# Five layer norms kept in PSUM with the modulation products spread around them, and the differential layer's copies and squares moved to ScalarE

## The reference

```python
def layer_norm(x, g, b):
    mu = jnp.mean(xf, axis=-1, keepdims=True)
    var = jnp.mean(jnp.square(xf - mu), axis=-1, keepdims=True)
    y = (xf - mu) * lax.rsqrt(var + LN_EPS) * g + b
...
h = layer_norm(DEEPNORM_ALPHA * h + mix, ln1_g[l], ln1_b[l])
h = layer_norm(DEEPNORM_ALPHA * h + ffn, ln2_g[l], ln2_b[l])
```

```python
a = (p[:, :, 0] - lam * p[:, :, 1]).astype(v.dtype)
o = jnp.einsum("bhqk,bkhd->bqhd", a, v)
...
return (rms_norm(o, subln_g) * (1.0 - lambda_init)).reshape(b, n, MIX_WIDTH)
```

## Time and profile before

| | |
|---|---|
| median of three runs | 2504.39 us (2498.84 to 2504.63) |
| the profiled execution | 2501.55 us, its span 2499.4 us |
| busy: TensorE, weight loads | 2202.2 us (88%), 1843.3 us (74%) |
| busy: VectorE, ScalarE, GpSimd | 1386.3 (55%), 987.7 (40%), 943.4 us (38%) |
| mean granted TensorE clock | 0.932 of full |
| read from HBM | 259.43 MB |

### The profile page before, as it was taken

One profiled execution on the slowest core, in us unless ns is written; L12 is line 12 of the kernel. 1 busy time (PEld: TensorE's weight loads), 2 busy tenths in 40 slices (PEclk: granted clock), 3 DMA queues, 4 the chain that ended last, 5 costly groups with the idle time before them and its releaser, 6 DMA issues.

```text
span 2499.4 us, 39552 instructions
## 1 busy us (share of the span) xinstructions
PE 2202.2 (88%) x14736; PEld 1843.3 (74%) x14736; DVE 1386.3 (55%) x2808; ACT 987.7 (40%) x1827; POOL 943.4 (38%) x588
## 2 busy tenths in 40 slices
PE   6969699978797998899998999999899888788898
PEld 5868699977787998667766966776687555566677
DVE  5694456458744664356652145556216788842666
ACT  4434456343434654533323243333325333224333
POOL 2444387025444840333422133332214333232343
PEclk8979899988998999889989999999999899988898
DMA  6433466553334665311132221113232111223111
GB/s 217 152 93 108 154 194 194 170 170 117 102 127 160 194 186 186 118 34 35 43 101 95 92 84 55 56 60 100 63 103 91 43 34 34 68 85 117 53 60 60
DMA packets 72848, 262.92 MB, mean 105 GB/s; under 512 B 8032, under 2 KB 10208, under 8 KB 72416
## 3 DMA queue, kind: packets, MB, share of 16 engines
q1 hardware_dynamic: 71392, 256.31, 32.4%
q0 software_dynamic: 1280, 4.20, 0.5%
HBM read 259.43 MB, written 1.05 MB: 104 GB/s over the span
## 4 chain that ended last, share of the span: by engine, by line
PE 64%; DVE 19%; issue 6%; ACT 5%; POOL 5%; DMA 1%; DVEq 0%; ACTq 0%; SPq 0%; POOLq 0%
PE gemm L401 13%; PE gemm L402 12%; PE gemm L403 12%; PE gemm L653 6%; PE score L692 5%; DVE r L1251 3%; PE obank L724 3%; PE tbank L622 3%; DVE d L1197 2%; PE stat L633 1%; DVE small L1457 1%; POOL arena L1768 1%; PE obank L728 1%; POOL w_lo L291 1%; DVE zt L1163 1%
## 5 line engine op out<-in xcount | busy, mean ns | idle before, releaser
L291 POOL TENSOR_TENSOR w_lo<-ring,w_hi 128x1024 fp32r<-128x1024 f32 x252 | 606.9, 2412 | 464.8 <-ACT w_hi L837 463.4
L401 PE MATMUL gemm<-g_hi,w_hi 128*128 128x256 f32 x1344 | 389.8, 290 | 42.2 <-POOL w_lo L291 38.2
L401 PE MATMUL gemm<-h_hi,w_hi 128*128 128x512 f32 (+1 forms) x928 | 388.8, 419 | 10.8 <-DVE h_lo L1562 8.1
L837 ACT ACTIVATE w_hi<-ring 128x1024 fp32r<-128x1024 f32 x344 | 362.1, 1054 | 86.2 <-PE gemm L403 34.2
L402 PE MATMUL gemm<-g_lo,w_hi 128*128 128x256 f32 x1344 | 381.9, 284 | 0.0
L403 PE MATMUL gemm<-g_hi,w_lo 128*128 128x256 f32 x1344 | 381.5, 284 | 0.0
L402 PE MATMUL gemm<-h_lo,w_hi 128*128 128x512 f32 (+1 forms) x928 | 352.8, 380 | 0.0
L403 PE MATMUL gemm<-h_hi,w_lo 128*128 128x512 f32 (+1 forms) x928 | 352.3, 380 | 0.0
L1108 ACT ACTIVATE pr<-score,small 128x512 f32<-128x512 f32 (+1 forms) x192 | 128.1, 669 | 464.4 <-DVE small L1459 464.4
L401 PEld LDWEIGHTS gemm<-g_hi,w_hi 128*128 128x128 f32 x1344 | 262.9, 196 | 55.9 <-POOL w_lo L291 45.6
L401 PEld LDWEIGHTS gemm<-h_hi,w_hi 128*128 128x128 f32 x928 | 180.3, 194 | 148.2 <-issue 109.4
(11 more groups left out here) (264 smaller groups left out, 3927.0 us busy)
## 6 DMA issues: line engine op xcount, KB each, us to landing
ring<-wall SPq DMA_DIRECT2D x478, 512.0 KB, 3.7
r<-nbias POOLq DMA_DIRECT2D x16, 256.0 KB, 3.0
cst<-consts SPq DMA_DIRECT2D x1, 2340.5 KB, 10.1
r<-x_t SPq DMA_DIRECT2D x1, 1024.0 KB, 4.9
x<-ctx_t SPq DMA_DIRECT2D x1, 1024.0 KB, 15.3
y_t<-x SPq DMA_DIRECT2D x4, 256.0 KB, 2.3
d<-pos SPq DMA_DIRECT2D x1, 128.0 KB, 10.0
```

Source lines behind the costliest of these rows:

```text
L291: eng.tensor_tensor(w_lo[:, q % SPLITS, :, :], ring[:, t % RING, :, :], w_hi[:, q % SPLITS, :, :].bitcast(F), ALU.subtract)\
L401: pe.matmul(out, w[0][:, k, :], x[0], start=start, stop=False)
L837: act.activation(w_hi[:, q % SPLITS, :, :], ring[:, t % RING, :, :], ACT.Copy).then_inc(S["hi_ready"], 1)
```

## The change

In the first four norms the next projection's first two tiles come before the eight modulation tiles in the order, so that they are split before the norm. TensorE does two modulation tiles ahead of the squares' sums and six in one piece behind them, then the first three chunks, and turns both rows only after these. ScalarE loads one table set with Ln and Exp ahead of the squares; it copies both rows out after the high parts, writes `x2` in GpSimd's place (whose `stream` is gone), and turns to the first eviction after that. VectorE writes factor times centred value to PSUM (`nrm`: the two score banks, the turning bank and the mean's bank), and makes each piece's low part right behind the next piece's factor; one refining step is moved ahead of `rstd_ready`. The last norm has no projection behind it and keeps its tiles in one place.

In layer C ScalarE copies the turned probabilities to `pt` (`keys`), squares and sums the output with a scale of 2 to the -32 in the same instruction (`output_squares`), and scales it (`subln`). The two clamps are dropped; the three small steps on the four sums and the product with the mask go to GpSimd's `subln_pow`. In layers A and C, and for context units of B, the scaled maximum is formed by one tensor_scalar per column instead of one scalar_tensor_tensor.

```diff
+    def after_norm(i, name, l, kinds):
+
+        nonlocal plan
+        plan += kinds[:2] + "RRRR" * FILL[i]
+        at[name, l] = len(plan) - 2
+        plan += kinds[2:]
...
+        def ada_rows(r):
+
+            return (pr[:, 1:3, :] if r < sum(FILL) else shf)[0:2, r % 2, :]
+
+        def nrm(m):
+
+            return (sbk[0], sbk[1], tb, st)[m % 4][:, (m // 4) * T:(m // 4) * T + T]
...
+            def layer_norm(i, first=None):
+
+                h = lambda k: (g_hi[:, k, :], g_lo[:, k, :])
+                at = n["tile"]
+                if first:
+                    n["tile"] += 2
+                ada = (_ for r in range(FILL[i]) for _ in ada_row())
+
+                def ada_part(steps):
+                    for _ in range(steps):
+                        next(ada, None)
...
-                fill(1)
+                ada_part(2 * KC)
                 for m in range(KC):
                     pe.wait_ge(S["squared"], i * KC + m + 1)
                     ins = pe.matmul(ob[:, 0:T], cw("ones_d"), sq8[:, m, :], start=(m == 0), stop=(m == KC - 1))
                 ins.then_inc(S["var_ready"], 1)
-                fill(FILL[i] - 1)
-                if i < 2 * DEPTH:
-                    n["h"] += 1
+                if not first:
+                    run(ada)
+                    for _ in range(FILL[i]):
+                        ada_columns()
+                    return
+                n["h"] += 1
+                run(ada)
+                run(chunk(h, T, h_wait, at))
+                run(chunk(h, T, None, at + 1))
+                run(chunk(h, T))
+                for _ in range(FILL[i]):
+                    ada_columns()
...
+            def ada_columns_all(rows):
+
+                act.wait_ge(S["bank_read"], n["g"])
+                for _ in range(rows):
                     ada_columns_out()
 
-            def layer_norm(i, b_name):
+            def layer_norm(i, b_name, first=True):
+
+                act.preload_act_table_set("natural_log_exp_and_others")
+                if first:
+                    n["tile"] += 2
+                    hi_parts(n["tile"] - 1)
                 for m in range(KC):
                     act.wait_ge(S["centred"], i * KC + m + 1)
                     act.activation(sq8[:, m, :], d1[:, m, :], ACT.Square).then_inc(S["squared"], 1)
-                fill(1)
                 act.wait_ge(S["var_ready"], i + 1)
                 seq(act.activation(lnv[:, 0:T], ob[:, 0:T], ACT.Ln, bias=EPC[:, 0:1]))
+                act.sem_inc(S["var_read"], 1)
                 seq(act.activation(rstd[:, 0:T], lnv[:, 0:T], ACT.Exp, scale=-0.5))
                 act.activation(zh[:, 0, 0:T], rstd[:, 0:T], ACT.Square).then_inc(S["rstd_ready"], 1)
-                fill(FILL[i] - 1)
                 for m in range(KC):
                     act.wait_ge(S["normed"], i * KC + m + 1)
-                    if i < 2 * DEPTH:
-                        act.activation(g_hi[:, m, :], d1[:, m, :], ACT.Identity, bias=cc(b_name, m)).then_inc(S["h_hi_ready"], 1)
+                    if first:
+                        act.activation(g_hi[:, m, :], nrm(m), ACT.Identity, bias=cc(b_name, m)).then_inc(S["h_hi_ready"], 1)
                     else:
                         act.activation(x2[:, m, 0:T], d1[:, m, :], ACT.Identity, bias=cc(b_name, m)).then_inc(S["h_full"], 1)
+                for _ in range(FILL[i]):
+                    ada_row_out()
+                if first:
+                    act.wait_ge(S["h_ready"], (i + 1) * KC)
+                    for m in range(KC):
+                        act.activation(x2[:, m, 0:T], nrm(m), ACT.Identity, bias=cc(b_name, m)).then_inc(S["h_full"], 1)
+                else:
+                    ada_columns_all(FILL[i])
...
+                        b = op(0, early + v) if j == 0 else op()
                         e = 2 * (J % 3) + v
                         if J >= 3:
                             act.wait_ge(S["ff_ready"], J - 2)
                         act.activation(fst[:, e, :], b[:, 0:T], ACT.Identity, bias=cc(f"ffn_b{l}", v * FC + j),
                                        scale=cc(f"ffn_w{l}", 3 * (v * FC + j) + 2)).then_inc(S["ff_evac"], 1)
+                        if j == 1 and v == 0:
+                            ada_columns_all(FILL[1 + 2 * l])
...
+                def keys(c, u):
+
+                    nonlocal turned_n
+                    turned_n += 1
+                    act.wait_ge(S["t_ready"], turned_n)
+                    act.activation(pt[:, (c * NU + u) // 2 % 2, :], tb[:, :], ACT.Copy).then_inc(S["t_read"], 1)
+
+                def output_squares(c):
+
+                    act.wait_ge(S["osb_full"], c + 1)
+                    for t in range(4):
+                        ins = act.activation(sq[:, 1, t * P:(t + 1) * P], osb[:, c % 2, t, :], ACT.Square, scale=2.0 ** -32, accum_out=OSS[:, t:t + 1])
+                    ins.then_inc(S["oss_ready"], 1)
+
+                def subln(c):
+
+                    nonlocal turned_n
+                    turned_n += 1
+                    act.wait_ge(S["ors_ready"], c + 1)
+                    for t in range(4):
+                        ins = act.activation(osb[:, c % 2, t, :], osb[:, c % 2, t, :], ACT.Copy, scale=ORS[:, t:t + 1])
+                    ins.then_inc(S["osb_ready"], 1)
...
+                        if kind == "C":
+                            past = [(c, u)] + past[:3]
+                            if past[lags] and closes(kind, us[past[lags][1]]):
+                                keys(*past[lags])
+                            if past[lags + 1] and past[lags + 1][1] == NU - 1:
+                                output_squares(past[lags + 1][0])
+                            if u == OT - 1 and c:
+                                subln(c - 1)
...
-                dve.wait_ge(S["squared"], (i + 1) * KC)
+                dve.wait_ge(S["var_read"], i + 1)
+                x, rs = st[:, 0:T], ob[:, T:2 * T]
+                seq(dve.tensor_scalar(x, ob[:, 0:T], LN_EPS, None, ALU.add))
                 dve.wait_ge(S["rstd_ready"], i + 1)
-                refine(rstd[:, 0:T], zh[:, 0, 0:T], ob[:, 0:T], 1.0, LN_EPS)
-                for m in range(KC):
-                    dve.scalar_tensor_tensor(d1[:, m, :], d1[:, m, :], cc(g_name, m), rstd[:, 0:T], ALU.mult, ALU.mult)\
-                        .then_inc(S["normed"], 1)
-                if b_name is None:
-                    return
-                split_to(AT["ln", i] + 4 * FILL[i] + 1)
-                for m in range(KC):
+                seq(dve.scalar_tensor_tensor(x, zh[:, 0, 0:T], -0.5, x, ALU.mult, ALU.mult))
+                seq(dve.scalar_tensor_tensor(rs, x, 1.5, rstd[:, 0:T], ALU.add, ALU.mult))
+
+                def low(m):
                     dve.wait_ge(S["h_hi_ready"], n["h"] * KC + m + 1)
-                    dve.scalar_tensor_tensor(g_lo[:, m, :], d1[:, m, :], cc(b_name, m), g_hi[:, m, :].bitcast(F), ALU.add, ALU.subtract)\
+                    dve.scalar_tensor_tensor(g_lo[:, m, :], nrm(m), cc(b_name, m), g_hi[:, m, :].bitcast(F), ALU.add, ALU.subtract)\
                         .then_inc(S["h_ready"], 1)
-                n["h"] += 1
+                for m in range(KC):
+                    dve.scalar_tensor_tensor(nrm(m) if b_name else d1[:, m, :], d1[:, m, :], cc(g_name, m), rs, ALU.mult, ALU.mult).then_inc(S["normed"], 1)
+                    if b_name and m:
+                        low(m - 1)
+                if b_name:
+                    low(KC - 1)
+                    n["h"] += 1
...
-                    rq = RQ[:, 8 * (c % 2) + 2 * t + hh:8 * (c % 2) + 2 * t + hh + 2 * w - 1:2]
-                    dve.scalar_tensor_tensor(NBm[:, i2:i2 + w], MX[:, i2:i2 + w], -1.0, rq, ALU.mult, ALU.mult).then_inc(S["s_max"], 1)
+                    for q in range(w):
+                        ins = dve.tensor_scalar(NBm[:, i2 + q:i2 + q + 1], MX[:, i2 + q:i2 + q + 1], rqc(t + q), -1.0, ALU.mult, ALU.mult)
+                    ins.then_inc(S["s_max"], 1)
...
-                pool.tensor_tensor(ORS[:, :], OSP[:, :], PW[:, 0:4], ALU.pow).then_inc(S["ors_ready"], 1)
+                seq(pool.tensor_scalar(OSP, OSS, 2.0 ** 64, 2.0 ** 64 / P, ALU.min, ALU.mult))
+                seq(pool.tensor_scalar(OSP, OSP, EPS, None, ALU.add))
+                seq(pool.tensor_tensor(ORS[:, :], OSP[:, :], PW[:, 0:4], ALU.pow))
+                seq(pool.tensor_scalar(OSM, OSS, 2.0 ** 64, None, ALU.is_lt))
+                pool.tensor_tensor(ORS, ORS, OSM, ALU.mult).then_inc(S["ors_ready"], 1)
```

137 lines of the change are left out of this document (56 added, 81 removed).

## The result

The changed kernel takes 2470.52 us (median of four runs, 2464.39 to 2474.51) against 2503.72 us (four runs, 2498.84 to 2504.63): ratio 0.9869, 95% interval 0.9843 to 0.9895. Timed again later on, its median was 2462.81 us, the ratio 0.9833 (0.9799 to 0.9866). The profiled execution took 2464.39 us, 37.2 less than that of before.

What follows compares the result with a forecast made beforehand. TensorE's queue was taken to set the end, with VectorE the bound in layer C, the differential layer. Norms 27.2 plus layer C 33.0 gave 60.2 us off the profiled 2501.55: 2441 us, range 2423 to 2464.

Steps and rivals of the forecast that it cites:

- M: In each layer norm, the time at which TensorE's mean products end; the forecast counts later steps from it, in us.
- chunk 2 after one more weight copy at 312.3, its bank free 313.3 after VectorE's two taps, chunk 3 ends 316.1: Norm ahead of layer 0's feed-forward: chunk 3 waits for chunk 2's bank; gain of 7.7 us claimed.
- of 6.1 us gained at chunk 0 the queue behind takes back 5.2: 0.9: First norm: late splitting and a cold start leave 6.1 us at chunk 0, of which 0.9 us remains as gain.
- Rival E: Whole kernel: no change, 2504 us; late bank gives back the norms' gain, layer C stays on the rotation; chance 0.04.
- moved chain: Layer C's output copy, squares, power and scaling over VectorE, ScalarE and GpSimd: 5.9 us, in time with 1.4 to spare.
- the remaining wait: Layer C, each chunk: TensorE's wait for the rotation's last addition, slowed beside GpSimd's weight split; 1.5 us stay.
- rival A: Layer C's chain through GpSimd is late, q's eviction 2.4 us late seven times: 17 us less gain, 2458; chance 0.13.
- rival B: A norm's tiles go one by one, 1.44 us each instead of 0.9: 4.3 us in four norms, 2458; chance 0.10.
- 24.5 + 1.5 = 26.0; six chunks: Layer C: TensorE's 24.5 us plus a 1.5 us wait bind each chunk, 26.0 instead of 30.26; gain 25.6 us.
- chunk 7: Layer C's last chunk, bound by VectorE, which splits the gated tiles there: gain 5.5 us of a possible 8.1.
- the tail: End of layer C: squares, power and scaling become 5.2 us instead of 7.1, gain 1.9 us.
- Rival C: Layer C: VectorE and GpSimd meet less, so the 1.5 us go as well: 9 us more gain, 2432; chance 0.10.

Runs made afterwards that it cites:

- run 3: Changed kernel with the eight x2 copies of each of the four early norms on VectorE instead of ScalarE: ratio 0.9757 to the kernel before.
- run 8: Changed kernel with each of the eight ScalarE x2 copies in a norm made twice: ratio 0.9889 to the kernel before.
- run 12: Changed kernel with the two modulation-row turnings behind the fifth instead of third up-projection chunk in both feed-forward layers: ratio 0.9817 to the kernel before.
- run 9: Changed kernel; in the differential layer weight parts made one tile further ahead, GpSimd's split behind the rotation's addition: ratio 0.9803 to the kernel before.
- run 11: The changed kernel measured again with nothing altered: ratio 0.9833 to the kernel before, span 2462.0 us.
- run 2: The kernel before with only the differential layer's part of the change: ratio 0.9884 to the kernel before, span 2475.8 us.
- run 4: Changed kernel; in the differential layer GpSimd's split comes behind the rotation's addition and the reciprocal root: ratio 0.9870 to the kernel before.

## Why the prediction was wrong

The direction and both mechanisms were right; the sum was 23.0 us too large against the profiled execution, and the four runs' median lies another 6.1 above that execution, where I had added nothing.

**Norms, 9.8 of the 23.0 us.** I take the norm ahead of layer 0's feed-forward. The steps up to the factor held: variance at M + 4.7 (forecast M + 4.6), factor M + 7.2 (M + 7.0), one table load, no row wait; a pair of VectorE's steps took 0.78 us (0.9). The first eviction at M + 22.7 (M + 22.4), after chunk 2 began, agrees partly by luck. Chunk 0's end was 1.8 us late, for a modulation tile's transfer and the lower clock, and ScalarE's second weight copy stood 1.29 us for it, a wait that the forecast did not have; the queue itself was 1.0 shorter than I had priced it (the x2 copies 3.0 for 3.3). In the heads of layer 1, where that wait was 2.61, the first eviction came 0.9 us later than forecast. The step that failed is "chunk 2 after one more weight copy at 312.3, its bank free 313.3 after VectorE's two taps, chunk 3 ends 316.1", M + 29.0. It ended at M + 31.1: its bank was 0.6 late (M + 26.9 for M + 26.2), and it ran at the lower clock, 4.3 us for the 2.8 I had taken. Before the change chunks 1 to 4 followed one another without a wait, 2.72 us each. By the eighth chunk another 0.7 us had gone. The same two terms stand in the heads of layer 1: chunk 3 starts at M + 27.3 and ends at M + 31.8, against M + 28.8 forecast.
What holds the bank is the queue that I had listed myself, with eight x2 copies ahead of the first eviction. Runs 3 and 8 price them at 4.2 us a norm when taken away and 3.5 when doubled, more than their own 3.0; with them away chunk 3 also ran at full clock in all four norms. Run 12 shows 2.5 us of the chain through the two turnings.
In the first norm "of 6.1 us gained at chunk 0 the queue behind takes back 5.2: 0.9" was the same step, off by more: it lost 2.0 in this profile, 3.5 on the average of seven. With the copies on VectorE it gains 1.2. Ahead of layer 1's feed-forward the gain was 7.3 of 7.7 us; there the kernel before had run its sums at the low clock, for which the forecast had allowed up to 1.7 more.
Rival E had named this mechanism ("the bank freed late by the x2 copies gives back all of the norms") and was given 0.04, as all or nothing. The norms fell short by over a third of their 27.2 us; how much of this is the bank alone is not shown, as the clock goes with it.

**Layer C, 8.1 of the 23.0 us.** The moved chain came to 5.7 us from VectorE's last copy to the end of the scaling (forecast 5.9): tiny GpSimd steps 0.20 to 0.25 (0.33), squares 1.3 (1.7). The addition took 2.70 (2.82), the remaining wait was 1.76 (1.5); the turning waited for nothing, so rival A is out, and rival B too (a pair of VectorE's steps in a norm took 0.78 us, not 1.44, and three products of chunk 0 came about 0.6 us apart, not 1.4). VectorE came to 18.7 us, not 17.5: operations that stand beside GpSimd's grew, as L1573 with 1.49 for 0.49.
The step that failed is "24.5 + 1.5 = 26.0; six chunks": 24.5 was read in chunk 1, at clock 0.97 and nearly without low-clock products, though the row of another chunk showed 0.94. With the wait that stays, the clock still falls behind four of its five occurrences, at 1.55 us each, 6.2 us in all. The six chunks take 26.93 us on average: 6 x 0.93 = 5.6 us too much (chunk 6, which has less work, hides the rest). Run 9 shows the other side: no wait, no low clock. Layer C's other 2.6 us are chunk 7 (3.8 for 5.5) and the tail (0.9 for 1.9); in chunk 7 TensorE waits 4.9 us for ScalarE's second modulation row, 3.6 before.
Rival C's gain, nine more in layer C, is what run 9 reached there (11.0), by an edit; the change as it stands never got there.

**The other 5.1 us** went in code that was not touched: 3.0 in block 1, 2.1 in the last layer. 2.0 of them are the down projection of layer 0, whose 18 chunks took 2.83 us each instead of 2.72, at a granted clock of 1.00 in both; in the kernel before, 15 chunks of the first heads had the slower pace instead. Its cause is open. The change does not fix where it falls: the same kernel again (run 11) had 2.72 there and 2.83 in the down projection of layer 1. The forecast had no term for this and its range no room.

## What to carry to other kernels

When a wait ahead of a stage is taken away, write out who stands in the evicting engine's queue in front of the first eviction, and hand each bank to each taker in program order, small ones included, until the steady pace is reached; moved copies belong on an engine that idles there (run 3), or perhaps behind the first evictions, which no run tried. Ask too which copies in that queue wait for a buffer that the first chunk must give back. Price a stage at the clock that it will have with the waits that remain, not at that of its quietest piece. Ask of two engines side by side what their operands are, not what the operation is called.

## What the runs showed of the hardware

- A VectorE operation with two SBUF sources beside a GpSimd split ends after the split in either form (2.70 us, against 0.68 apart); one with a PSUM source takes 0.48 beside it too. A tensor_scalar with a single SBUF tile as its source is held as well: L1577 took 2.42 us beside two splits and 0.35 apart (run 9), L1573 1.49 beside GpSimd's product for z and 0.49 apart.
- A wait of about 1.76 us was followed by 3.4 us at the 1.2 GHz level in four of five like chunks, the same four in this kernel and its repeat, and in five of five in run 2; a wait of 2.76 us at another point of the chunk (run 4) in none. Waits of 1.96 and 1.97 us ahead of the same chunk of two norms (run 12) were followed by it once. So the length of the wait alone does not decide.
- In the pairs of a norm VectorE's low part took 0.48 us with its source tile in SBUF or in PSUM. The Trainium skill ("VectorE: DVE Perf Modes", the TRN2 errata section) has 62 more cycles for the latter; the measurement decides.
- A stretch of 18 chunks can run 4% slower than the same chunks in another run at the same granted clock (2.83 and 2.72 us).
